# A two-block transformer kernel: a router computed ahead of its norm, 8 KB expert rows, and a final norm applied after the turn

## The chip, the cores and the metric

The kernel runs on one core of a Trainium2 chip. The metric is device time in microseconds (us) of one execution. Engines are named PE (TensorE), DVE (VectorE), ACT (ScalarE) and SP (SyncE, which issues nearly all loads here). POOL does nothing in this kernel.

## The reference, cut to what matters

256 tokens of width 1024, all in float32. A first block has two layers of FFN, three kinds of attention, and FFN. A second block normalizes and modulates, runs attention and retention, and adds the result through `w_out`. What the change touches comes after that:

```
x_new = x + gt1 * (concat([attn_x, ret_x]) @ w_out)
h2 = rmsnorm(x_new, norm2_g) * (1 + sc2) + sh2            # modulated norm
grp_p  = softmax(h2 @ w_grp + b_grp)                      # 4 groups, the best is taken
sel    = (h2 @ w_exp + b_exp) of that group's 8 experts   # 32 experts in all
p_e, j = top_k(softmax(sel), 2)                           # two experts for each token
weights = p_g * p_e / sum(p_e)
y = sum over the two: weight * (silu(h @ w_gate[e]) * (h @ w_up[e])) @ w_down[e]
out = rmsnorm(x_new + gt2 * y, final_norm_g)
```

Each expert has `w_gate` and `w_up` of 1024 x 512 and `w_down` of 512 x 1024, 2 MB each, 201 MB for all 32.

## The kernel before

Activations stand turned, features on partitions: `xT` is 128 x 8 tiles x 256 tokens. Weights come as pieces in a fixed order (`stream_plan`), which SP loads in `stream` (L537 to L561) and PE takes with `take` (L648). Before the experts a piece is 512 KB and there are six places in `W`. From the experts on, `piece_place` gives a ring of 24 places of 512 KB (`RING`): 14 of them over `W`, `WH` and `WL`, which the earlier stages use, and 10 behind the zone. SP fills the ring once ahead of the routing in `first_experts` (L523), as each place comes free. Every further load waits until PE has used the piece 24 places back (`plain_used`), and for the table of which expert each block of 64 slots belongs to (`table_ready`, L598). SP reads an expert's number into a register at its first gate piece (L553).

A gate or up piece holds two of the eight rows of 512 values that each partition needs, 4 KB in one run; a down piece holds 128 rows of 1024 values, 4 KB a partition.

PE, ACT and DVE share four PSUM banks in turns: PE's `begin` waits until DVE gave the bank four turns back, `take` on DVE waits for PE's product (`work_ready`), and `give` frees it. `link` makes DVE wait for its own last operation. Four other banks hold sums over a whole product.

The router's order is serial. All of w_out2's products end, `residual` (L1629) adds them to x, ACT squares (L1279), PE sums over partitions with a matrix of ones (`norm`, L734), ACT takes the root, DVE the reciprocal (L1613) over 256 columns, and 8 + 8 operations (L1616, L1626) scale and shift to `hT`. PE multiplies `hT` with the router's matrix `WR` (L1083, 16 matmuls of 36 columns, each run as two records) and turns `hT` to tokens on partitions (L1091). DVE routes each half of 128 tokens by itself (L2046 to L2083), with an exponential on ACT between (L1484, L1486). Then DVE makes `h2l`, the low part of the turned h2 (L2088), PE counts the tokens of each expert (L1098 to L1103), and DVE works out the blocks of each expert, the expert table (L2115 to L2122), the slot of each token (L2124 to L2139) and the selection matrices of the first four blocks (`select`, L2141). PE gathers the tokens of four blocks with them (`gather`, L1106), DVE copies to `XT` (L2165), and PE turns the weighted selection (`turn_selection`).

The experts run in 16 pairs of blocks. For each pair PE computes gate and up products (`hidden_product`, L1137), adds the pair before back to the tokens in two parts (`scatter`, L1129), turns the hidden values, gathers the next four blocks on every second pair, and computes the down product (`down_product`, L1160). Two blocks of 64 slots lie side by side on PE's columns. Eight more blocks are run only if the table asks for them; in this data it does not.

At the end DVE waits for the last scatter, reads the table's length for the branch (L2197), and goes through residual, norm and scaling to `hT`. PE turns it (L1218), DVE copies four tiles (L2204), and SP stores each (L606).

## Time and profile before

| | |
|---|---|
| median of 3 runs | 2227.05 us (2223.64 to 2229.04) |
| the profiled execution | 2220.84 us, its span 2218.9 us |
| mean granted PE clock | 0.979 |
| PE busy | 2090.0 us (94%), modelled |
| PE weight loads | 1694.3 us (76%) |
| DVE busy | 1187.9 us (54%) |
| ACT busy | 632.8 us (29%) |
| loaded from memory | 467.96 MB |
| DMA packets | 287144, of which 223188 under 2 KB and 286988 under 8 KB |

A busy PE is not PE at its peak: matmuls are pipelined and their ends are modelled, so a wait for data shows only in part. The page's slices show where the load on the DMA engines is; the chain of waits shows what ended last. A share of the DMA just above 1 means that packets overlap on an engine.

### The profile page before, as it was taken

The numbers are of one execution on the slowest core, as the hardware profiler recorded it, in microseconds if no ns is written. First come the engines' busy times: TensorE is split into PE (matmuls) and PEld (weight loads), VectorE is DVE, ScalarE is ACT, GpSimd is POOL, SyncE is SP. The second block draws the span as 40 slices with busy tenths as digits, with TensorE's granted clock in tenths as the row PEclk, the third lists the DMA queues.
The fourth block names the chain that finished last, engine by engine and source line by source line (L and its number), as shares of the span: only waits on it lengthen the run. The fifth ranks groups of instructions, "written<-read, shape, count | busy, mean of one in ns | idle before, by whom it ended". The sixth has DMA issues, their size and how long they took to land.

```text
span 2218.9 us, 33949 instructions
## 1 busy us (share of the span) xinstructions
PE 2090.0 (94%) x14045; PEld 1694.3 (76%) x14045; DVE 1187.9 (54%) x2050; ACT 632.8 (29%) x934; POOL 0.2 (0%) x4
## 2 busy tenths in 40 slices
PE   7999999999999999999999999979893999999997
PEld 7999998779999999999878999968573444334443
DVE  6665658774655655666885555553556222222212
ACT  4433434423333533344441433320321000000000
POOL 0000000000000000000000000000000000000000
PEclk9999999999999999999999999989996999999999
DMA  7966552238866666654233676512321899999994
GB/s 227 281 204 181 169 166 84 86 114 225 263 211 195 196 212 204 181 171 152 67 114 106 229 234 210 164 39 76 133 103 69 333 416 416 415 416 415 416 417 186
DMA packets 287144, 471.36 MB, mean 212 GB/s; under 512 B 17306, under 2 KB 223188, under 8 KB 286988
## 3 DMA queue, kind: packets, MB, share of 16 engines
q1 hardware_dynamic: 285680, 466.19, 61.3%
q10 hardware_dynamic: 1308, 2.96, 0.5%
q8 instruction: 114, 1.87, 0.3%
q14 instruction: 42, 0.34, 0.0%
HBM read 467.96 MB, written 1.13 MB: 211 GB/s over the span
## 4 chain that ended last, share of the span: by engine, by line
PE 82%; DMA 10%; DVE 5%; ACT 1%; issue 1%; SPq 1%; DVEq 0%; ACTq 0%
PE ps L618 81%; DMA ring_zone<-in_moe_w_up_dram 5%; DMA ring_over<-in_moe_w_gate_dram 4%; DMA W<-in_ffn_w_gate_dram 1%; PE ps L903 1%; DVE QK L1838 1%; SPq L556 0%; PE ps L1038 0%; DVE hl L1564 0%; DVE hT L1616 0%; DVE WL L1553 0%; DVE xT L1571 0%; DMA PT<-in_norm_g_dram 0%; PE ps L1156 0%; ACT WH L1243 0%
## 5 line engine op out<-in xcount | busy, mean ns | idle before, releaser
L1553 DVE TENSOR_TENSOR WL<-W,WH 128x1024 fp32r<-128x1024 f32 x372 | 453.0, 1223 | 341.9 <-ACT WH L1243 341.9
L618 PE MATMUL ps<-hh,WH 128*128 128x256 f32 x2128 | 610.1, 287 | 12.2 <-DVE WL L1553 6.6
L618 PE MATMUL ps<-hh,WL 128*128 128x256 f32 x2128 | 601.5, 283 | 0.0
L618 PE MATMUL ps<-hl,WH 128*128 128x256 f32 x2128 | 601.4, 283 | 0.0
L1243 ACT ACTIVATE WH<-W 128x1024 fp32r<-128x1024 f32 x372 | 391.5, 1056 | 496.8 <-PE ps L618 472.6
L618 PEld LDWEIGHTS ps<-hh,WH 128*128 128x128 f32 x2128 | 403.0, 189 | 33.0 <-issue 30.1
L618 PEld LDWEIGHTS ps<-hl,WH 128*128 128x128 f32 x2128 | 402.8, 189 | 0.2
L618 PEld LDWEIGHTS ps<-hh,WL 128*128 128x128 f32 x2128 | 402.8, 189 | 0.0
L618 PE MATMUL ps<-ring_over,XT 128*64 128x512 f32 x896 | 204.7, 596 | 24.4 <-DMA ring_over<-in_moe_w_up_dram 13.3
L618 PE MATMUL ps<-hid_h,WH 128*128 128x256 f32 x704 | 202.9, 288 | 0.0
L618 PE MATMUL ps<-hid_h,WL 128*128 128x256 f32 x704 | 198.7, 282 | 0.0
L618 PE MATMUL ps<-hid_l,WH 128*128 128x256 f32 x704 | 198.5, 282 | 0.0
L618 PEld LDWEIGHTS ps<-ring_over,XT 128*64 128x64 f32 x896 | 65.2, 136 | 160.9 <-issue 159.7
L1501 ACT ACTIVATE sgE<-ps 128x512 f32<-128x512 f32 x16 | 9.6, 597 | 464.0 <-PE ps L618 464.0
L618 PEld LDWEIGHTS ps<-hid_h,WH 128*128 128x128 f32 x704 | 132.9, 189 | 6.3 <-issue 5.8
L618 PEld LDWEIGHTS ps<-hid_l,WH 128*128 128x128 f32 x704 | 132.7, 189 | 0.5
L618 PEld LDWEIGHTS ps<-hid_h,WL 128*128 128x128 f32 x704 | 132.7, 188 | 0.0
L2183 DVE TENSOR_TENSOR hidE<-sgE,ps 128x512 f32<-128x512 f32 x16 | 11.0, 687 | 217.3 <-PE ps L618 217.3
L618 PE MATMUL ps<-yT,W 128*128 128x256 f32 x512 | 116.2, 380 | 0.0
L618 PE MATMUL ps<-ring_zone,hidT 128*64 128x512 f32 x512 | 113.5, 595 | 0.6 <-issue 0.6
L618 PEld LDWEIGHTS ps<-yT,W 128*128 128x128 f32 x512 | 95.0, 190 | 14.4 <-issue 2.8
L618 PEld LDWEIGHTS ps<-ring_zone,hidT 128*64 128x64 f32 x512 | 35.8, 137 | 67.2 <-issue 67.2
(315 smaller groups left out, 2338.4 us busy)
## 6 DMA issues: line engine op xcount, KB each, us to landing
ring_over<-in_moe_w_gate_dram SPq DMA_DIRECT2D x128, 512.0 KB, 14.8
ring_zone<-in_moe_w_down_dram SPq DMA_DIRECT2D x128, 512.0 KB, 15.1
ring_over<-in_moe_w_up_dram SPq DMA_DIRECT2D x96, 512.0 KB, 15.4
W<-in_ffn_w_gate_dram SPq DMA_DIRECT2D x88, 512.0 KB, 5.0
W<-in_ffn_w_up_dram SPq DMA_DIRECT2D x88, 512.0 KB, 4.0
W<-in_ffn_w_down_dram SPq DMA_DIRECT2D x88, 512.0 KB, 3.7
W<-in_w_in_dram SPq DMA_DIRECT2D x78, 512.0 KB, 3.9
W<-in_w_gate_dram SPq DMA_DIRECT2D x48, 512.0 KB, 3.6
```

The costliest lines, as they stand in the source:

```text
L618: ins = nc.tensor.matmul(o, lhsT, rhs, start=start, stop=stop, skip_group_check=True, **kw)
L903: ins = nc.tensor.transpose(bank[:, k * T + q * P:k * T + (q + 1) * P], S[:, u % 4, q * T + k * P:q * T + (k + 1) * P], ident)
L1243: nc.scalar.activation(high, W[:, i % RAW, :], ACT.Copy).then_inc(high_ready, 1)
L1501: nc.scalar.activation(sgE[:, :], bank, ACT.Silu).then_inc(sg_ready, 1)
L1553: v.tensor_tensor(low, W[:, i % RAW, :], high.bitcast(F32), ALU.subtract).then_inc(low_ready, 1)
L1838: give(v.reciprocal(r2, r2))
L2183: v.tensor_tensor(hidE[:, :], sgE[:, :], bank, ALU.mult).then_inc(work_free, 2)
```

## The change

Three parts are changed at once.

**Router.** The norm factor of a token is one number, so the logits can be computed from x before it is known: `logit = r * (x_new @ (G * WR)) + (shift @ WR + b)`. `G` is the column gain of the norm and its modulation. The last term, `LB`, is computed early, beside the first projections. `logits_and_squares` is put between w_out2's products: for the two feature tiles of each PSUM bank it adds 2 matmuls for the logits (turned, 64 columns each, on two column strips) and 2 for the squares (32 columns each, on four strips), as soon as DVE has added that bank to x. A small product with `fold` adds the strips and turns the logits; one-column products with `ones` turn the sum of squares, so the root and reciprocal are over 2 values a partition. ACT scales x to `hT` without the factor; the factor is applied when ACT and DVE copy the turned tiles to `h2h` and `h2l`, and the shift when DVE copies the gathered tiles to `XT`. The shift (`MOD[:, 24:32]`) is needed with the features in another order, and goes through a DRAM scratch. Routing runs both halves of the tokens in one operation where the form allows. The exponentials and weights (`routing_weights`), the expert table (`block_table`) and the weighted half of the selection (`select_weighted`) are moved behind the first gather; the turning of the first weighted selection is moved behind the first pair's hidden values.

**Expert rows.** A piece is 1 MB: four of a partition's eight rows of gate or up (8 KB in one run), or two of its four rows of down, whose rows are now dealt `(p k)` instead of `(k p)`. `hidE` is written in the matching order. The ring has 12 places of 1 MB, 7 of them over the earlier buffers.

**End.** The last scatter signals each PSUM bank, DVE adds and scales bank by bank without the norm factor, PE turns the tiles meanwhile, and the factor is applied by DVE (first half of the tokens) and ACT (second) in the copy out of PSUM.

```
-RING, RING_OVER = 24, 14
+LONG = 2 * PIECE
+RING, RING_OVER, RING_RAW = 12, 7, RAW // 2
...
-            plan.extend((kind, 2 * pair + e, j, 0) for j in range(4) for e in range(2))
+            plan.extend((kind, 2 * pair + e, j, 0) for j in range(2) for e in range(2))
...
-                return w.rearrange("o (p k) n -> p (o k) n", k=KD)[:, 2 * c:2 * c + 2, :]
+                return w.rearrange("o (p k) n -> p (o k) n", k=KD)[:, 4 * c:4 * c + 4, :]
             elif kind == "moe_down":
-                return I["moe_w_down_2"][0, bass.ds(key, 1)].rearrange("o (k p) n -> p (o k) n", p=P)[:, c:c + 1, :]
+                w = I["moe_w_down_2"][0, bass.ds(key, 1)]
+                return w.rearrange("o (p k) n -> p (o k) n", k=HIDDEN)[:, 2 * c:2 * c + 2, :]
...
                     if plan[i] == ("w_in2", 0, 0, 0):
                         sp.dma_start(moe_const[:, :], I["consts"][:, CONST_MOE:]).then_inc(moe_load, 16)
+                        sp.wait_ge(m_ready, KD * DEPTH)
+                        sp.dma_start(mod_scr.rearrange("(k p) -> p k", p=P), MOD[:, 24:32, 0], allow_slow_non_contiguous=True)\
+                            .then_inc(shift_scr, 16)
+                    if plan[i] == ("w_in2", 0, 5, 0):
+                        sp.wait_ge(shift_scr, 16)
+                        sp.dma_start(shift_of[:, :], mod_scr.rearrange("(p k) -> p k", k=KD)).then_inc(shift_load, 16)
...
+            bank = begin()
+            for k in range(KD):
+                mm(bank[0:1, 0:40], MOD[:, 24 + k, 0:1], WR[:, k, :], k == 0, k == KD - 1,
+                   then=work_ready if k == KD - 1 else None)
+            turns.step()
...
+            def logits_and_squares(b):
+
+                if b == 0:
+                    pe.wait_ge(wg_ready, 1)
+                    pe.wait_ge(work_free, turns.n)
+                pe.wait_ge(x2_ready, b + 1)
+                for k in (2 * b, 2 * b + 1):
+                    at = k % 2 * 64
+                    mm(ps[at:at + 64, 0, 0:T], WG[:, k, :], xT[:, k, :], k < 2, k >= KD - 2,
+                       then=lg_ready if k == KD - 1 else None)
+                pe.wait_ge(sq_ready, due(sq_ready))
+                for k in (2 * b, 2 * b + 1):
+                    at = k % 4 * 32
+                    mm(squares[at:at + 32, 0:T], ones[:, 0:32], mT[:, k, :], k < 4, k >= 4,
+                       then=sum_ready if k == KD - 1 else None)
...
                     done_plain()
-            norm()
+                    if half and c:
+                        logits_and_squares(c - 1)
+            logits_and_squares(3)
+            pe.wait_ge(part_ready, due(part_ready))
+            for tt in range(TT):
+                mm(ps[:, 1, tt:tt + 1], rs[:, tt * P:(tt + 1) * P], ones[:, 0:1], tt == 0, tt == 1,
+                   then=sum_ready if tt else None)
+            pe.wait_ge(lc_ready, 1)
+            for tt in range(TT):
+                mm(ps[:, 2, tt * 64:tt * 64 + 40], rstd[:, tt * P:(tt + 1) * P], fold[:, :], tt == 0, tt == 1,
+                   then=lg_ready if tt else None)
...
             def select(quad):
 
+                link(v.tensor_scalar(near[:, :, :], token_slot[:, :, :], float(-QUAD * SLOTS * quad), None, ALU.add))
+                for tt in range(TT):
+                    ins = v.tensor_scalar(Sel_a[:, tt, :], slot_no, near[:, tt, 0:1], None, ALU.is_equal)
+                link(ins)
+                for tt in range(TT):
+                    ins = v.scalar_tensor_tensor(out=Sel[:, tt, :], in0=slot_no, scalar=near[:, tt, 1:2],
+                                                 in1=Sel_a[:, tt, :], op0=ALU.is_equal, op1=ALU.add)
+                ins.then_inc(sel_ready, 1)
...
             def gathered(quad):
 
                 for g in range(4):
                     bank = take()
-                    give(v.tensor_copy(flat(XT[:, quad % 2, 2 * g:2 * g + 2, :]), bank))
+                    for k in (2 * g, 2 * g + 1):
+                        ins = v.tensor_scalar(XT[:, quad % 2, k, :], bank[:, k % 2 * T:(k % 2 + 1) * T],
+                                              shift_of[:, k:k + 1], None, ALU.add)
+                    give(ins)
...
                 select(first // QUAD)
                 gathered(first // QUAD)
-                selection_turned(first // 2)
+                if first == 0:
+                    block_table()
+                    routing_weights()
+                select_weighted(first // QUAD)
...
+            for b in range(4):
+                dve.wait_ge(acc_ready, accs + b + 1)
+                for f in range(2):
+                    k = 2 * b + f
+                    ins = v.scalar_tensor_tensor(out=xT[:, k, :], in0=ps[:, b, f * T:(f + 1) * T],
+                                                 scalar=MOD[:, 40 + k, 0:1], in1=xT[:, k, :],
+                                                 op0=ALU.mult, op1=ALU.add)
+                ins.then_inc(last_x, 1)
+                dve.wait_ge(last_x, b + 1)
+                for k in (2 * b, 2 * b + 1):
+                    ins = v.tensor_scalar(hT[:, k, :], xT[:, k, :], col("final2", k), None, ALU.mult)
+                ins.then_inc(last_scaled, 1)
+            dve.wait_ge(std_ready, 1)
+            v.reciprocal(lamt[:, 0:TT], rstd_of[:, :]).then_inc(last_norm, 1)
+            dve.wait_ge(rows_ready, 2)
+            dve.wait_ge(last_norm, 1)
+            for q in range(2):
+                v.tensor_scalar(otok[:, 0, q * 512:(q + 1) * 512], ps[:, WORK + q, :], lamt[:, 0:1], None, ALU.mult)\
+                    .then_inc(otile, 1)
```

In the routing that replaces L2046 to L2083, DVE's order is: 2 operations `LGE = ps * rtok + LB`; maximum, its index (each for both halves), a cast, the group's one-hot, the product with it and its sum over groups; maximum and index again, a cast, the experts' one-hots, their sum, `chosen`, and two subtractions for the exponentials. Then come `h2l` and the counts as before. The slots take `first`, `own_at`, `slot[:, 0]` in two steps, and two each of pick, reduce and unshift. PE counts with 3 matmuls instead of 5. On PE the first product of a group of four blocks waits for each `XT` bank by itself (`dve_did(x_idx - 3 + k // 2)`) instead of for the last.

## Rows read from the trace of the kernel before

**Rows 1.** The page's slices of 55.5 us, GB/s loaded and stored in each.

```profile
GB/s 227 281 204 181 169 166 84 86 114 225 263 211 195 196 212 204 181 171 152 67 114 106 229 234 210 164 39 76 133 103 69 333 416 416 415 416 415 416 417 186
```

**Rows 2.** Four stretches: busy time, PE clock, DMA share, GB/s.

```profile
1520.00:1560.00 40.00, 40.00 (x185) 34.85 (x184) 7.18 (x11) 0.00 (x0) 0.00 (x0) 1.00 0.24 79
1680.00:1685.00 5.00, 4.88 (x23) 4.88 (x24) 0.06 (x1) 0.00 (x0) 0.00 (x0) 0.50 0.00 0
1690.00:1727.00 37.00, 12.47 (x65) 9.60 (x66) 25.87 (x103) 4.36 (x11) 0.00 (x0) 0.63 0.00 1
1879.00:1940.00 61.00, 55.92 (x269) 24.61 (x268) 14.22 (x34) 1.20 (x2) 0.00 (x0) 1.00 1.03 416
```

**Rows 3.** The chain that ended last, its end: start, us, what.

```profile
2165.01 14.95 DMA ring_zone<-in_moe_w_up_dram
2180.09 3.86 PE ps L618 x16
...
2194.13 3.71 PE ps L618 x16
```

**Rows 4.** PE's timeline, the first down products: start, us, what.

```profile
1739.75 7.09 PE L618 MATMUL ps<-ring_zone,hidT 128*64 128x512 f32 x32 [0.61 <-issue]
...
1768.63 7.09 PE L618 MATMUL ps<-ring_zone,hidT 128*64 128x512 f32 x32
...
1793.69 7.09 PE L618 MATMUL ps<-ring_zone,hidT 128*64 128x512 f32 x32
```

**Rows 5.** Timeline of all engines, 1655 to 1760, from residual to first expert product.

```profile
1666.80 3.23 DVE L1640 SCALAR_TENSOR_TENSOR xT<-ps,MOD,xT 128x256 f32<-128x256 f32 x8 [15.54 <-PE ps L618]
1667.71 0.63 ACT L1279 ACTIVATE mT<-xT 128x512 f32<-128x512 f32 x1 [27.17 <-DVE xT L1640]
...
1672.21 0.47 ACT L1287 ACTIVATE rs<-ps,eps 128x256 f32<-128x256 f32 x1 [1.52 <-PE ps L618]
...
1672.79 1.75 DVE L1613 RECIPROCAL rstd<-rs 128x256 f32<-128x256 f32 x1 [2.76 <-ACT rs L1287]
...
1680.12 7.04 PE L618 MATMUL ps<-WR,hT 128*128 128x36 f32 x32 [7.94 <-DVE hT L1626]
...
1687.19 0.16 DVE L2042 TENSOR_TENSOR LG<-ps,rb 128x4 f32<-128x4 f32 x1 [7.13 <-PE ps L618]
...
1698.14 2.48 DVE L2088 TENSOR_TENSOR h2l<-ps,h2h 128x512 fp32r<-128x512 f32 x4
...
1701.32 0.19 DVE L2095 TENSOR_SCALAR blocks<-ps 128x32 f32<-128x32 f32 x1 [0.56 <-PE ps L618]
...
1704.27 1.48 DVE L2115 TENSOR_TENSOR XT<-scan,moe_const 1x1280 f32<-1x1280 f32 x1
...
1707.65 0.18 DVE L2124 TENSOR_TENSOR first<-scan,blocks 128x32 f32<-128x32 f32 x1
...
1711.24 0.17 DVE L2144 TENSOR_SCALAR near<-token_slot 128x4 f32<-128x4 f32 x1
...
1716.72 0.79 PE L618 MATMUL ps<-Sel,h2h 128*128 128x256 f32 x2 [15.44 <-DVE SelW L2156]
...
1723.42 12.24 PE L618 MATMUL ps<-ring_over,XT 128*64 128x512 f32 x56 [0.56 <-DVE XT L2165]
```

**Rows 6.** SP's queue, the first loads that need the table.

```profile
1727.27 5.49 SPq L556 DMA_DIRECT2D ring_over<-in_moe_w_gate_dram  x8
```

**Rows 7.** Timeline of the end, 2160 to 2219.

```profile
2199.34 3.23 DVE L1640 SCALAR_TENSOR_TENSOR xT<-ps,MOD,xT 128x256 f32<-128x256 f32 x8 [5.36 <-issue]
...
2213.86 2.89 SPq L606 DMA_DIRECT2D out_dram<-mT  x4
...
2215.70 0.69 DVE L2204 COPY mT<-ps 128x512 f32<-128x512 f32 x1 [0.16 <-PE ps L1218]
```

**Rows 8.** Timelines of the second block's first norm and of w_out2.

```profile
1452.32 6.52 PE L618 MATMUL ps<-mT,ones 128*128 128x256 f32 x16 [3.24 <-ACT mT L1279]
...
1638.97 27.79 PE L618 MATMUL ps<-yT,W 128*128 128x256 f32 x128
```

More of the change, by code:

```diff
@@ L1007, in _ @@
                     side(kind, piece)
+                if g == 8:
+                    pe.wait_ge(lrow_ready, 1)
+                    bank = begin()
+                    mm(bank[:, 0:40], ones[0:1, :], lrow[:, :], True, True, then=work_ready)
+                    turns.step()
             t_idx, pv_idx = {}, {}
@@ L1073, in _ @@
                                yT[:, k, :], half + f + j == 0, k == KD - 1,
-                               then=acc_ready if half and c == 3 and f and j == 3 else None)
+                               then=acc_ready if half and f and j == 3 else None)
                     done_plain()
-            norm()
-            pe.wait_ge(h_ready, due(h_ready, KD))
-            bank = begin()
-            for tt in range(TT):
-                for k in range(KD):
-                    last = tt == TT - 1 and k == KD - 1
-                    mm(bank[:, tt * 64:tt * 64 + 36], hT[:, k, tt * P:(tt + 1) * P], WR[:, k, :],
-                       k == 0, k == KD - 1, then=work_ready if last else None)
-            turns.step()
+                    if half and c:
[9 more added lines that the diff above has]
+                   then=lg_ready if tt else None)
+            pe.wait_ge(h_ready, due(h_ready, KD))
             for j in range(4):
@@ L1191, in experts @@
                     t_idx = turn_hidden()
+                    if pair == first // 2:
+                        turn_selection(pair)
                     if y_idx is not None:
@@ L1409, in _ @@
             turns.step(4)
+            turns.step()
             norm(xT)
@@ L1442, in _ @@
                     side(kind, piece)
+                turns.step(g == 8)
             def decay(h):
@@ L1496, in experts @@
                 turns.step(4)
-                turns.step()
                 for pair in range(first // 2, last // 2):
@@ L1502, in experts @@
                     turns.step(3)
+                    turns.step(pair == first // 2)
                     if more and pair % 2 == 1:
@@ L1896, in _ @@
                 v.tensor_copy(rt[:, 0, b:b + 1], eps[:, :]).then_inc(x_tiles, 1)
+            bank = take()
+            give(v.tensor_copy(lrow[:, :], bank[0:1, 0:40]))
+            given()
+            v.tensor_copy(rt[:, 1, 0:1], eps[:, :]).then_inc(lrow_ready, 1)
             link(scaled(xT[:, :, :], hT[:, :, :]))
@@ L1971, in _ @@
                     side(kind, piece)
+                if g == 8:
+                    bank = take()
+                    give(v.tensor_tensor(LB[:, :], bank[:, 0:40], rb[:, :], ALU.add))
+                    given()
             def decay_arg(h):
```

409 lines of the change are left out of this document (259 added, 150 removed).

## The prediction

> **What bounds the kernel now.** I read the slices of the page first: from slice 33 to slice 39 the core loads 415 to 417 GB/s without a break [rows 1]. The table by stage says how close that is to full: in a stretch of 61 us the DMA share is 1.03 at 416 GB/s while TensorE's modelled busy time is 55.9 us [rows 2]. The chain of waits then shows that the DMA really ends last: it runs through the landing of a piece in each pair, the last one 14.95 us long to 2179.96, and PE works only the last 16 matmul records after it [rows 3]. PE alone could go faster: with pieces in store, three starts of the down product lie 28.88 and 25.06 us apart, 53.9 us a quad against 61 us by DMA [rows 4]. So the expert stage is worth its bytes divided by the rate, plus what lies in front of it and behind it. In front: from the end of the w_out2 products (1666.8) to the first expert product (1723.42) is 56.6 us of one serial chain [rows 5], and between 1690 and 1727 the DMA share is 0.00 [rows 2], since the ring is full and no slot comes free before PE eats a piece; the first new issue is at 1727.27 [rows 6]. A microsecond saved in that chain is therefore a microsecond of the end. Behind: from the last scatter (2194.13 + 3.71 = 2197.84) to 2218.9 is 21.1 us of small steps [rows 3, 7].
>
> **The sum is made against the profiled execution,** 2220.84 us (span 2218.9); the median of the three runs is 2227.05, so 6.2 us are added at the end, by subtracting the saving from the median.
>
> **Router, before.** 56.6 us [rows 5]: 13.3 us of residual, squares, factor and norm to 1680.12; 7.0 us for 16 logit matmuls (32 records); 10.95 us for the routing of two token halves (1687.19 to 1698.14, some 54 short DVE operations, 0.20 us each with the two ACT trips); 3.2 us of h2l; 2.95 us of block counts; 3.4 us of expert table; 3.6 us of slots (16 operations, 0.22 each); 5.5 us of selection; 6.7 us of gather with the last XT copy.
>
> **Router, after.** (a) The residual, squares and logits of bank b now follow w_out2's own bank b. Two groups (b = 0, 1) stand in PE's queue ahead of the last w_out2 products. A group is 4 matmuls; a w_out2 matmul of the same 256 columns is 27.79/64 = 0.43 us [rows 8]; the four sit on separate column strips, as the expert products do, which take 12.24/28 = 0.44 us for 512 columns [rows 5], half of what 0.43 at 256 gives. So 0.9 us a group (1.7 if strips don't overlap), +1.8 us. The group b = 2 lies beside the residual of bank 3. (b) From there to the logits: 2 residual operations 0.85 (3.23/8 each [rows 5]), square 0.7, two ones products 0.55, copy out 0.55, two one-column products 0.6, root 0.35, reciprocal and wait 0.35, with sizes from the steps they replace: together 4.1 us, between 3 and 6. The 1.75 us reciprocal over 256 columns, the 16 norm operations and the 7.0 us of logits are gone. (c) Routing is 22 operations with both halves in each step, at 0.20 us: 4.5 us (3.3 if unlinked neighbours overlap). The exponentials leave the path. (d) h2l still stands ahead of the counts on DVE, 3.2 us; counts 2.95. PE's transposes and ACT's four scaled copies lie beside the routing; without that cover 2 us more. (e) The table moves behind the gather: 0 here. (f) Slots 10 operations at 0.22: 2.2 us. (g) Selection is one `near` and four operations of 256 columns near 0.42 us (the same STT costs 0.40 on PSUM [rows 5]): 1.9 us, as the weighted half is moved behind the gather too. (h) Gather 5.9 us [rows 5]; the product starts on the first XT banks, so the last copy is not waited for. Sum: 1.8 + 4.1 + 4.5 + 3.2 + 2.95 + 2.2 + 1.9 + 5.9 = 26.6 us. **Saving 30 us,** between 26 and 33. The granted clock was 0.50 in this stretch [rows 2], the 1.2 GHz level; the gather's price contains it, and I count on no better.
>
> **What the move costs.** SP waits for the table, which DVE now makes after the XT copies: about 1.0 + 3.4 us after the product's start, and a slot of 1 MB comes free only after 8 products (3.5 us) instead of 4. Issue today is 3.85 us after the start (1723.42 to 1727.27 [rows 5, 6]), of which 1.75 is the products, so about 2 is SP's own way. After: 4.4 + 2 = 6.4 us. SP then gives 2 MB at once where before it gave 0.5 MB pieces, so of these 2.6 us I count 1.4 (0 to 3). Nothing but expert loads is queued there. The routing weights and the weighted selection (some 6 us of DVE) must be ready for the transposition of the first pair, 14 us after the start: hidden. The bias row adds 8 products with one stationary column ahead of the norm at 1452.32, whose 6.52 us are on the path [rows 8]; the bound is 16 records at 0.22 us = 3.5, the least near 0.5: +2, and 0.4 for the second small product. The shift's way through DRAM is 8 elements a partition while SP is several pieces ahead: 0 (1 at most).
>
> **The 8 KB rows.** The stream from restart to the last up piece brings 352 pieces of 0.52 MB, 184.5 MB; counted from 1730.6, where a full-rate stream would have had to begin, to 2179.96 [rows 3] it is 449.4 us. What does a longer row give? At 4 KB rows a full share carries 416/1.03 = 404 GB/s; in a stretch with 1 KB rows alone, 79 GB/s at 0.24, it is 329 [rows 2]. With 16 engines that is 162 ns and 50 ns a packet, so 37.5 ns a KB and 12 ns fixed; 8 KB would take 312 ns instead of 324, 3.8% less. That is one bound (16.4 us); the other is no gain, if 416 is already what the port takes. I take 2.6%, two thirds of the way, as the fixed part was seen between 1 and 4 KB and nothing shows it gone: **11.4 us.** PE's 53.9 us a quad stay under the 59.5 that this gives.
>
> The Trainium skill (DMA: Bandwidth & Descriptors, Why small descriptors are slow) puts the fixed cost at about 3 fabric cycles a packet, and its ceiling is 435 GB/s. By it 4 KB to 8 KB gives 1.2%, 5 us, and a time near 2188; the trace's 12 ns a packet speaks for more than 3 cycles.
>
> **Tail of the stream.** After the last up pieces land PE has 8 products instead of 4: +1.75 us; against it the down product today waits 0.5 us for its last piece and won't: +1.3.
>
> **The end, before:** 21.1 us: 1.5 until DVE starts at 2199.34, then residual, squares, root, reciprocal, scaling, transposes and copies one behind another to 2216.4, four issues of 0.72, and 2.15 from the last issue (2216.75) to the end of the span [rows 7]. **After:** the branch on the table is taken while PE scatters, and acc is given bank by bank, so DVE starts 2.3 us before the scatter ends and does a bank in 1.5 us: the last x is ready 2.9 us after it; square 0.7, squares product 0.6, copy 0.6, small products 0.6, transposes of the last bank 0.9: 6.4; scaled copy 0.75; the third and fourth issue follow at 0.72 steps to 9.4; from there to the end 2.5: 11.9. **Saving 9 us** (7 to 10).
>
> **Total:** -30 + 1.4 + 2.4 - 11.4 + 1.3 - 9 = -45.3. 2227.05 - 45.3 = 2181.8, say **2182 us** (profiled near 2175.5).
>
> **Rivals.**
> 1. The rate doesn't rise (packets are cut to 4 KB, or 416 is the port): 2182 + 11.4 = 2193. For it: the flat 415 to 417 [rows 1] looks like a ceiling. Against: the price per packet above. 18%.
> 2. The coarser ring makes PE and DMA take turns. With 12 slots of 1 MB, each pair does 4 more products after its last up piece; if that delays the reissue on which the stream hangs, 16 pairs lose 1.75 us each, 28 us: 2210. Against: in the 10 us that PE is behind, some 4.5 MB land of 12.6, so the queue never runs dry. 7%.
> 3. The other side, slower: the long rows are served worse than 4 KB ones, as one engine now holds each piece up for longer. All else being won (33.9 us), this decides from 449.4/(449.4 + 33.9) = 0.93 of the rate, 387 GB/s; at 380 GB/s it is 2236. No row shows a longer row going slower; 1 KB to 4 KB went the other way [rows 2]. 3%.
> 4. More than forecast (3.8% and a router at 24 us): 2166. 4%.
>
> My own case holds 68%, 2170 to 2190. **Range** 2170 to 2197: it takes in rival 1 and leaves out 2, 3 and 4. All but rival 3 are faster by over 0.3% (6.7 us, about what three runs here can tell from no change): faster 0.96, same 0.01, slower 0.03.
>
> **What the profile would show.** Right: first expert product 25 to 29 us after the last w_out2 product; LGE within 5 us of it; GB/s near 427 over whole slices and packets of 8 KB; last store about 12 us after the last scatter. Wrong: GB/s still 416; SP's first table-dependent issue over 8 us after the first product; PE idle on DMA for longer than now with the DMA share under 1; a wait of the counts on h2h.

## The result, and the profile after

The changed kernel takes 2166.61 us, the median of 4 runs (2160.68 to 2170.63), against 2226.98 us (4 runs, 2223.64 to 2229.04) for the kernel before beside it: a ratio of 0.9727, 95% interval 0.9706 to 0.9749. It is faster by 60.4 us. The forecast was 45 us, 2182, and its range ended at 2170. The profiled execution took 2166.41 us; its span, 2164.6, is 54.3 us shorter than before's. The other 6 us of the 60.4 are not in the two profiles: before's profiled execution (2220.84) was 6.2 us under its own median, and under every other execution of that kernel on record (2221.03 to 2231.11), while after's is at its median. Where a good part of them went is shown behind experiment 15.

The stages, from the two traces (us):

| stretch | before | after | difference | forecast |
|---|---|---|---|---|
| start to the end of the first block | 1446.6 | 1435.7 | -10.9 | 0 |
| to the start of w_out2's products | 192.4 | 194.5 | +2.1 | +2.4 |
| w_out2's start to the first expert product | 84.5 | 53.6 | -30.8 | -30 |
| first expert product to the last `hidE` | 458.7 | 453.0 | -5.7 | -8.7 |
| to the end of the last scatter | 15.7 | 15.5 | -0.2 | 0 |
| last scatter to the end | 21.1 | 12.2 | -8.9 | -9 |

The stream is the stretch from the first expert product to the last `hidE`; its forecast is -11.4 for the rows, +1.4 for the restart and +1.3 for the tail. Two rows are not as forecast, in opposite directions: the first block gave 10.9 us that nobody had asked for, and the stream gave 3 less.

**The router.** The timeline of the changed kernel, all engines, answers to [rows 5]:

```profile
1656.95 3.72 PE L652 MATMUL ps<-yT,W 128*128 128x256 f32 x16
...
1660.71 0.88 DVE L2164 SCALAR_TENSOR_TENSOR xT<-ps,MOD,xT 128x256 f32<-128x256 f32 x2 [3.92 <-PE ps L652]
...
1661.74 0.65 PE L652 MATMUL ps<-xT,PT 128*64 128x256 f32 x4
...
1663.00 0.38 ACT L1575 ACTIVATE rs<-ps 128x256 f32<-128x256 f32 x1 [0.74 <-PE ps L652]
...
1664.63 0.43 DVE L2175 SCALAR_TENSOR_TENSOR LGE<-ps,rtok,LB 128x40 f32<-128x40 f32 x2
...
1668.47 2.60 DVE L2241 SCALAR_TENSOR_TENSOR h2l<-ps,rtok,h2h 128x512 fp32r<-128x512 f32 x4
...
1670.99 0.18 DVE L2248 TENSOR_SCALAR blocks<-ps 128x32 f32<-128x32 f32 x1
...
1673.93 0.19 DVE L2265 TENSOR_TENSOR first<-scan,blocks 128x32 f32<-128x32 f32 x1
...
1675.73 0.17 DVE L2325 TENSOR_SCALAR near<-token_slot 128x4 f32<-128x4 f32 x1
...
1677.52 0.80 PE L652 MATMUL ps<-Sel,h2h 128*128 128x256 f32 x2 [6.81 <-DVE Sel L2330]
...
1683.83 10.94 PE L652 MATMUL ps<-ring_over,XT 128*64 128x512 f32 x49
```

Read the starts one after another. From the last w_out2 product (1660.67) the last residual, squares, sums, root and reciprocal lead to `LGE` in 4.0 us (forecast 4.1). The routing of both halves together, up to `h2l`, is 3.84 us, where two halves one after the other were 10.95. Counts, slots and selection follow to 1677.52, and the gather to 1683.83 is 6.3 us. Before, the same stretch from w_out2's last product was 56.6 us; it is 23.2 now, and w_out2 itself grew from 27.79 to 30.46 us because the logits and squares of two banks stand among its products.

**The restart.** SP's queue, the first loads that need the table, answers to [rows 6]:

```profile
1689.39 3.40 SPq L581 DMA_DIRECT2D ring_over<-in_moe_w_gate_dram  x4
```

That is 5.56 us after the first product (1683.83), where it was 3.85.

**The stream.** The page's slices of loaded GB/s, the window of 61 us (as in [rows 2]), and the end of the chain that ended last (as in [rows 3]), all of the changed kernel:

```profile
GB/s 226 276 218 178 164 184 98 88 88 193 282 216 201 200 225 216 176 158 185 103 92 78 195 243 215 195 73 78 79 97 175 315 422 420 421 421 421 421 421 252
```

```profile
1879.00:1940.00 61.00, 55.84 (x274) 26.37 (x272) 16.36 (x39) 1.19 (x2) 0.00 (x0) 1.00 1.01 421
```

```profile
2108.00 24.93 DMA ring_zone<-in_moe_w_up_dram
2133.06 5.58 PE ps L652 x24
2139.08 8.77 PE ps L652 x40
...
2148.71 1.12 PE ps L652 x4
```

The rate rose from 416 to 421, not to 427. The last up piece now stands for 24.93 us in that chain instead of 14.95, and DMA is 17% of the chain instead of 10%: this stage is bound by DMA before and after. PE's part behind the last landing is 24 records instead of 16, as a coarser piece must leave.

**The end.** The timeline of the changed kernel's last 15 us, beside [rows 7]:

```profile
2149.85 0.88 DVE L2405 SCALAR_TENSOR_TENSOR xT<-ps,MOD,xT 128x256 f32<-128x256 f32 x2 [1.29 <-PE ps L652]
...
2157.70 0.38 ACT L1615 ACTIVATE rs<-ps 128x256 f32<-128x256 f32 x1 [2.00 <-PE ps L652]
...
2159.08 0.17 DVE L2414 RECIPROCAL lamt<-rstd_of 128x2 f32<-128x2 f32 x1 [3.39 <-ACT rstd_of L1617]
...
2160.13 1.88 SPq L640 DMA_DIRECT2D out_dram<-mT  x4
```

DVE starts on the first bank 2.55 us before the last scatter ends (2152.40), where before it waited for all of it, and the first store is issued 7.7 us behind the scatter instead of 16.0.

**The first block.** The diff puts nothing into it before the bias row. Yet three long unbroken stretches of PE, of the same count of records, are shorter. They stand in the chain that ended last; first the kernel before, then the changed one:

```profile
564.34 164.94 PE ps L618 x1421
734.79 204.58 PE ps L618 x1745
...
1193.48 252.55 PE ps L618 x1962
```

```profile
563.81 161.94 PE ps L652 x1421
731.26 201.13 PE ps L652 x1745
...
1186.19 248.89 PE ps L652 x1962
```

The windows over the first of them (busy times, clock, DMA share, GB/s), before and after:

```profile
564.40:729.00 164.60, 164.60 (x1421) 160.28 (x1422) 98.69 (x114) 61.98 (x63) 0.00 (x0) 1.00 0.71 218
```

```profile
564.00:725.00 161.00, 161.00 (x1417) 156.72 (x1417) 98.53 (x114) 61.99 (x63) 0.00 (x0) 1.00 0.73 223
```

PE never waits in either, the granted clock is 1.00 in both, and the DMA has room: so it is not a clock, a wait or a load. It is 3.0, 3.45 and 3.66 us, 1.4 to 1.8%, for the same instructions with the same operands. What did change for them is where their operands lie: the router's new small buffers are allocated in front of `hl`, and push `hl`, `hh` and everything in the zone 1184 B up in each partition. (`hh` and `hl` are the high and low part of the activations, which stream through PE as the moving operand; `WH` and `WL` are the same of the weights, the stationary operand; `hid_h` and `hid_l`, the hidden values, lie in the zone.) The experiments had to settle this, and why the stream gave less than forecast.

### The profile page after: what moved, and what is told of

It reads as the page before. It is cut to its first block, busy times and chain, and to the rows that moved or that the text cites. A ratio compares the mean times of both kernels' runs of the same rounds, so it can differ in the third digit from the quotient of the medians.

```text
span 2164.6 us, 33353 instructions
## 1 busy us (share of the span) xinstructions
PE 2062.4 (95%) x14055; PEld 1676.9 (77%) x14055; DVE 1181.1 (55%) x2009; ACT 637.2 (29%) x942; POOL 0.2 (0%) x4
## 4 chain that ended last, share of the span: by engine, by line
PE 77%; DMA 17%; DVE 4%; ACT 1%; issue 1%; SPq 0%; DVEq 0%; ACTq 0%
PE ps L652 75%; DMA ring_zone<-in_moe_w_up_dram 15%; DMA W<-in_ffn_w_gate_dram 2%; PE ps L937 1%; DVE QK L1949 1%; PE ps L1082 0%; DVE hl L1674 0%; DVE WL L1663 0%; DVE xT L1681 0%; ACT WH L1324 0%; DMA PT<-in_norm_g_dram 0%; SPq L581 0%; DVE xT L1726 0%; DVE yT L1952 0%; DVE xT L1861 0%
## 5 line engine op out<-in xcount | busy, mean ns | idle before, releaser
L1663 DVE TENSOR_TENSOR WL<-W,WH 128x1024 fp32r<-128x1024 f32 x372 | 453.0, 1223 | 337.7 <-ACT WH L1324 337.7
L652 PE MATMUL ps<-ring_over,XT 128*64 128x512 f32 x896 | 228.4, 595 | 30.2 <-DMA ring_zone<-in_moe_w_up_dram 13.6
L652 PEld LDWEIGHTS ps<-ring_over,XT 128*64 128x64 f32 x896 | 77.7, 137 | 174.9 <-issue 174.5
L2379 DVE TENSOR_TENSOR hidE<-sgE,ps 128x512 f32<-128x512 f32 x16 | 16.8, 1048 | 205.0 <-PE ps L652 205.0
L652 PE MATMUL ps<-yT,W 128*128 128x256 f32 x512 | 116.7, 381 | 0.0
```

The costliest lines, as they stand in the source:

```text
L652: ins = nc.tensor.matmul(o, lhsT, rhs, start=start, stop=stop, skip_group_check=True, **kw)
L1663: v.tensor_tensor(low, W[:, i % RAW, :], high.bitcast(F32), ALU.subtract).then_inc(low_ready, 1)
L2379: v.tensor_tensor(hidE[:, :].rearrange("p (k m) -> p m k", k=HIDDEN), by_row(sgE[:, :]), by_row(bank), ALU.mult).then_inc(work_free, 2)
```

## The experiments

"First block" ends at the reciprocal of its closing norm; "stream" is from the first expert product to the last `hidE`. Each ratio is to the kernel before on the same chip.

**1. The expert rows alone** (the kernel before with the second part of the change).

```
-RING, RING_OVER = 24, 14
...
+LONG = 2 * PIECE
+RING, RING_OVER, RING_RAW = 12, 7, RAW // 2
...
-                return w.rearrange("o (p k) n -> p (o k) n", k=KD)[:, 2 * c:2 * c + 2, :]
+                return w.rearrange("o (p k) n -> p (o k) n", k=KD)[:, 4 * c:4 * c + 4, :]
```

> The kernel before with the 8 KB expert rows and the ring of 12 places alone; router, end and all buffers in front of the zone are as before. Theory A (the rows are worth what the two traces show in that stage: rate 416 to 421 GB/s, first expert product to the last up piece landed 456.5 to about 448 us, tail 1.6 us longer): about 6 us faster, 2221 against 2227, first block unchanged (final_g norm starts at about 1446.6). Theory B (as predicted, 2.6% more rate): 9 to 10 us faster. Rival C (the coarse ring costs what the long rows give): within 2 us of before. If the first block gets 10 us faster here too, the ring or the piece order is what speeds it up.

Measured: 2216.02 us, ratio 0.9963 (0.9949 to 0.9977). The stream takes 448.6 us, 10.1 less than before, at these rates (the page's slices):

```profile
GB/s 223 276 207 187 165 171 86 86 103 208 274 212 192 199 215 203 180 166 169 77 86 114 201 247 214 189 31 84 144 38 134 271 425 425 425 425 425 426 425 192
```

So alone the rows gave more than in the full change, and more than the 8.7 net of the forecast. SP's first load came here 5.56 us after the first product too (1727.53 to this row of SP's queue), with the table still made early:

```profile
1733.09 3.40 SPq L559 DMA_DIRECT2D ring_over<-in_moe_w_gate_dram  x4
```

The later restart is therefore the coarser piece's, and not the moved table's.

**2. The end alone.**

```
-            residual(lambda k: MOD[:, 40 + k, 0:1], waited=True)
-            norm(xT, hT, lambda k: col("final2", k), last=True)
...
+            for b in range(4):
+                dve.wait_ge(acc_ready, accs + b + 1)
...
```

> The kernel before with the new end alone. Theory A: last scatter to the end of the span goes from 21.1 to about 12.2 us, 9 us faster, 2218, nothing else moves. Rival: part of the gain belongs to the shorter router (clock, DVE state), then under 7 us.

Measured: 2217.95 us, ratio 0.9966 (0.9952 to 0.9980). From the last scatter to the end 12.2 us against 21.1: the whole term, alone. The medians say 7.6 us, between 4.5 and 10.7 by the interval, which takes in the stage's 8.9.

**3. The change without the expert rows.**

```
-LONG = 2 * PIECE
-RING, RING_OVER, RING_RAW = 12, 7, RAW // 2
+RING, RING_OVER = 24, 14
```

> The changed kernel with the 4 KB rows and the ring of 24 places of before. Theory A (the parts add, and the first block's 10.9 us come with the buffers that the router part adds): about 2173, first block ends its last FFN at about 1435.7, router stretch about 31 us shorter than before, expert stream about 456 us as before. Rival C (rows cost or give nothing): 2167, as the changed kernel. Rival D (the first block's gain comes with the ring): 2184, first block as before.

Measured: 2179.41 us, ratio 0.9792 (0.9775 to 0.9808). From w_out2's start to the first expert product 53.6 us, end 12.2, first block 1436.2. But the stream is 467.4 us, longer than before's 458.7 although its loads are the same. The two surprises are both here, without the long rows. I had expected 456 us for the stream and 2173 in all.

**4. Only the places.** The kernel before with 294 unused floats in front of `hl`; not one instruction changes.

```
+        sb("pad", [P, 294])
         hl = sb("hl", [P, KD, T], FR)
```

> The kernel before with one unused buffer of 294 values a partition (1176 B) ahead of hl and the zone, which is the sum by which the changed kernel's new buffers move them. No instruction changes. Theory A (the place of hl, hh and the zone in the partition sets how fast PE reads, or how it collides with DVE and ACT): about 10 us faster, all in the first block's FFNs (1421 matmul records of the second FFN in 162 us instead of 165). Rival E (the first block's gain is a difference between executions, chips or the clock): no change, within 3 us of 2227. Rival F (it comes from something else in the changed program, such as the DRAM layout or the router's loads): no change either, but e3 shows it.

Measured: 2216.66 us, ratio 0.9958 (0.9943 to 0.9972): unused bytes make the kernel 9 us faster. The chain that ended last has the changed kernel's stretch:

```profile
563.76 161.93 PE ps L619 x1421
```

The first block is 1435.5 us, 11 shorter than in before's profile. The stream is 465.7 us, 7 longer, at this rate in the window of 61 us:

```profile
1879.00:1940.00 61.00, 55.16 (x266) 24.42 (x264) 14.20 (x34) 1.19 (x2) 0.00 (x0) 1.00 1.03 409
```

That settles both surprises as matters of place. The two stages together give only 4 us, though, where the medians (2216.66 and 2224.74) give 8 and the ratio 9. The rest is that before's profiled execution, 2220.84, was shorter than its runs beside this one.

**5 to 7. Which buffer, in small steps.** The kernel before: with 32 B in front of `hl` and the zone kept on its multiple of 256 B (it moves by a whole 256 B); with `hl` kept and the zone moved 32 B; with 64 B in front of all of them. One run each.

```
+        sb("pad", [P, 8])                       # 5, and 56 floats behind hl; 7: [P, 16]
         hl = sb("hl", [P, KD, T], FR)
+        sb("pad", [P, 8])                       # 6, behind hl
```

> The kernel before with hl alone moved by 32 B in the partition (so that it starts 32 B into a 64 B line) and everything behind it on 64 B lines as before. Theory A1 (the FFNs' gain comes from where PE's moving operand hl lies): the last FFN ends at about 1435 instead of 1446 to 1453, the expert stream keeps 458 to 459 us. Theory A2 (it comes from the zone, hh and the hidden values): first block as before, stream as before.

> The kernel before with the zone alone (hh, the hidden values, ring_zone) moved by 32 B, hl as before. Theory A2: last FFN ends near 1435 and the expert stream (first product to the last hidden product) is 465 to 467 us, since ring_zone is off its 64 B line. Theory A1: last FFN as before, 1446 to 1453, and the stream still 465 to 467 us. If both halves count, the FFN gain is split between this run and the one of hl.

> The kernel before with hl and the zone moved by 64 B, so that they stay on 64 B lines but leave the 256 B ones. If only the place within 64 B counts: first block as before (1446 to 1453) and stream 458 to 459 us. If the place within 256 B counts: a gain in the first block or a loss in the stream here too.

Measured: 2216.79, 2229.47 and 2208.05 us, beside 2224.59 (one run) for the kernel before. The stretch of 1421 records takes 163.87, 163.53 and 161.61 us (before 164.94), the first block 1444.3, 1449.3 and 1428.5. `hl` and the zone each have a part in it, as far as single runs tell. My theory behind these runs, that a start off a 64 B line makes the gain, fell: the move by 64 B keeps all on such lines and gains most. The stream is 458.4 us in the first, where `ring_zone` is back on a multiple of 256 B, and 465.8 and 464.4 in the others, where it is 32 and 64 B behind one.

**8. The changed kernel with `hl` and `ring_zone` on 64 B lines** (192 B behind a multiple of 256).

```
+        sb("pad", [P, 8])
         hl = sb("hl", [P, KD, T], FR)
```

> The changed kernel with 32 B of padding ahead of hl, so that hl and the zone lie on 64 B lines again. If the place within 64 B is the whole of it: last FFN ends at 1446 to 1451 instead of 1435.7 and the expert stream goes from 453.0 to 448.6 us, as with the rows alone (e1); in all some 7 us slower than the changed kernel, near 2173. Rival (the first block's gain needs only a move from where it was): still 1436, stream 448.6, near 2162.

Measured: 2171.59 us, one run. First block 1442.2 (the stretch of 1421: 163.37), stream 452.8. A line of 64 B does nothing for the stream either.

**9. The changed kernel with `ring_zone` on a multiple of 256 B.**

```
-            ("ring_zone", [P, RING - RING_OVER, LONG], F32))
+            ("pad", [P, 24], F32), ("ring_zone", [P, RING - RING_OVER, LONG], F32))
```

> The changed kernel with one difference: 96 unused bytes in front of ring_zone, so that the five ring places behind the zone begin on a multiple of 256 B in the partition. hl, hh and the zone stay where they are. Theory that the place of the DMA's destination sets the stream: from the first expert product to the last hidE it takes 448.6 us, as in the rows-only kernel, against 453.0 in the changed kernel; nothing else changes, first block 1435.7; time 4.4 us under the changed kernel, near 2162. Rival, that the lost 4.4 us belong to the router and end in the same kernel (more work on PE and DVE beside the stream): the stream stays at 453, time 2166.

Measured: 2158.76 us (4 runs), ratio 0.9709 (0.9687 to 0.9732). The stream is 448.3 us against 453.0, as the first theory said, and the slices show 425 GB/s as in experiment 1. In the medians the intervals of this kernel and the changed one overlap, so the gain rests on the stage. In this profile w_out2's start also comes 3.7 us sooner after the first block. That is the clock: from 1455 to 1630 us the granted clock is 0.95 here and 0.93 in the changed kernel, and 0.02 of 175 us are 3.5 us.

**10. Both places.** As 9, with `hl`, `hh` and the zone at the 64 B offset of experiment 7; the row `lrow` moves into an unused part of `rt`, so that it takes no place of its own.

```
-        lrow = sb("lrow", [1, 40])
+        lrow = rt[0:1, 14:16, :].rearrange("p a n -> p (a n)")[:, 0:40]
+        sb("pad_hl", [P, 16])
         hl = sb("hl", [P, KD, T], FR)
...
+            ("pad", [P, 48], F32), ("ring_zone", [P, RING - RING_OVER, LONG], F32))
```

> The changed kernel with its buffers placed by what the runs so far show: ring_zone on a multiple of 256 B, and hl, hh and the zone with the 64 B offset of the fastest first block seen. Theory, that both gains are of the places alone and add up: first block 1428.5 to 1430 (1435.7 in the changed kernel), stream 448.6, time 2154 to 2157. Rival, that the first block's time follows from something else that differed in that kernel: first block stays at 1435.7, time 2162.

Measured: 2155.16 us, ratio 0.9682 (0.9660 to 0.9703). The chain's stretch repeats experiment 7 to the hundredth:

```profile
565.43 161.61 PE ps L653 x1421
```

Stream 449.0. But the first block is 1432.6, only 1.2 below experiment 9 and 4 above experiment 7: TensorE's rate in these stretches is a matter of the places; the length of the whole block is not that alone (see behind experiment 15).

**11. Long pieces, short rows.** The kernel before with pieces of 1 MB and the ring of 12, each partition's bytes from two places in memory.

```
+                return w.rearrange("o (p a c i) n -> p (o a) c (i n)", a=2, c=2, i=2)[:, :, c, :]
...
+                return w.rearrange("o (k p) n -> p (o k) n", p=P)[:, 2 * c:2 * c + 2, :]
```

> The kernel before with the changed kernel's 1 MB pieces and its ring of 12, but each partition's bytes come as two runs of 4 KB from two places in memory, so packets stay at 4 KB. ring_zone is on a multiple of 256 B. Theory, that the length of the packet sets the rate: stream 458.7 us as before or a little more, since PE's grouping of four adds up to 1.4 us; time 2225 to 2227. Rival, that half as many DMA instructions and waits of SP make the gain: stream 448.6 us, time 2216. If the coarser ring had a price of its own (the rival of 7 per cent in the prediction), it shows here bare: over 462 us.

Measured: 2226.40 us, ratio 1.0010 (1.0000 to 1.0020), stream 459.1 us. Its page, slices and packets:

```profile
GB/s 224 274 213 180 162 170 86 86 105 215 272 209 191 206 211 207 176 168 161 68 107 111 217 238 212 170 38 76 132 91 80 319 417 416 416 416 416 416 417 190
DMA packets 284067, 471.31 MB, mean 212 GB/s; under 512 B 14234, under 2 KB 220116, under 8 KB 283916
```

Same pieces, same ring, same issues as experiment 1, which has 234764 packets under 8 KB: 416 instead of 425 GB/s. So the long packet, with the long run in memory that makes it, is the whole gain, and the coarse ring costs 0.4 us, nothing.

**12. All moved by 128 B.**

```
+        sb("pad", [P, 32])
         hl = sb("hl", [P, KD, T], FR)
```

> The kernel before with 128 unused bytes in front of hl, so that hl, hh, the zone and ring_zone all begin 128 B behind a multiple of 256 B. If the rate of the expert stream wants a destination on 256 B and not only on 128 B, the stream takes 464 to 466 us as with 64 B; if 128 B is enough, 458.5. For the first block, one more point on what the place does to matmuls: offsets of 0, 64 and 160 B gave 1446.6, 1428.5 and 1435.5 us. If it follows the distance to the weights' buffers (WH begins 128 B behind a multiple of 256), 128 B puts both on the same offset and gives an extreme, slower than 1446 or faster than 1430; if it is no matter of 256 B at all, something between.

Measured: 2234.88 us, ratio 1.0051 (1.0034 to 1.0069): 128 unused bytes make it 11 us slower. Stream 465.5, so 128 B is not enough for it; and the chain's stretch is the slowest of all:

```profile
569.46 166.11 PE ps L619 x1421
```

**13 to 15. Place or distance, and the other part of the ring.** All kernels so far have `W`, `WH`, `WL` and, over them, `ring_over` 128 B behind a multiple of 256. In 13 every buffer moves by 64 B; in 14 every buffer by 128 B, with `ring_zone` kept on its multiple; 15 does the same to the kernel of experiment 10.

```
+        sb("pad_all", [P, 32])                  # 16 in experiment 13
         with nc.sbuf_tensor("ring_over", [P, RING_OVER, PIECE], F32) as ring_over:
```

> The kernel before with 64 unused bytes in front of the first buffer, so that every buffer moves by 64 B and all distances stay. If TensorE's rate in the first block follows from the place of hl, hh and the zone alone, its stretch of 1421 records takes 161.6 us, as with the 64 B in front of hl; if it follows from their distance to WH and WL, 164.94 us as before. Stream: ring_zone and ring_over both off a multiple of 256 B (64 and 192), so 464 to 466 us if only that counts.

> The kernel before with 128 unused bytes in front of the first buffer and 128 more in front of ring_zone: ring_over and ring_zone now both begin on a multiple of 256 B, and hl, hh and the zone keep their distance to WH and WL. If distance counts for TensorE, the stretch of 1421 records takes 164.94 us; if place, 166.11 us. Stream, in the kernel before 458.7 us: if ring_over's 14 places cost by the same measure as ring_zone's 10 (7 us), it takes about 449 us and the time is 2214 with 164.94 or 2224 with 166.11; if loads over ring_over cost nothing by their place, 458.7.

> The kernel best_places with 128 more unused bytes in front of the first buffer, ring_zone staying on its multiple of 256 B: now ring_over is on one too, and hl is 192 B behind one, at the same distance to WH as in best_places. If distance counts for TensorE, the stretch of 1421 records stays at 161.61 us; if place, 163.4 us. Stream, 449.0 us in best_places: if ring_over's 7 of 12 places cost as ring_zone's 5 did (4.5 us), it falls by 6 us to 443, unless PE's own 53.9 us for four blocks or another limit shows first; time near 2149. If they cost nothing: 449, time 2155.

Measured: 2234.41 us (one run); 2219.01 us, ratio 0.9982 (0.9972 to 0.9991); 2145.15 us, ratio 0.9647 (0.9631 to 0.9663), the fastest kernel of this study and 3.5% under the kernel before. The chains' stretch in 13, 14 and 15:

```profile
567.92 165.05 PE ps L619 x1421
```

```profile
566.64 164.95 PE ps L619 x1421
```

```profile
556.81 161.61 PE ps L654 x1421
```

With all distances kept it is before's 164.94 again, wherever the buffers lie, and with experiment 10's distances 161.61. So TensorE's rate does not follow the place of `hl`, `hh` and the zone but their distance to the buffers in front of them. Of those PE reads only `WH` and `WL` in these stretches. That these two are the ones that count is argued; no run moved them alone.

One rival can be looked up in the traces: that PE collides with what DVE, ACT or the DMA write beside it. I took the time from the start of one of these matmuls to the start of the next, between 570 and 718 us, over some 1150 pairs in each trace (steps over 150 ns left out). The mean is 119.0 ns in the kernel before, 116.7 in the changed one, 116.6 in experiment 7 and 119.9 in experiment 12. Over the pairs beside which neither DVE nor ACT works (66 to 94 of them) it is 119.1, 117.3, 117.1 and 120.0; over those with no DMA packet under way (110 to 144), 119.0, 116.7, 116.4 and 120.0. So the difference is in PE's own pace and needs no other engine. The small moves show one thing more. In experiment 5 the step from a matmul that reads `hh` to one that reads `hl` fell most, from 118.8 to 116.4 ns; from `hl` to `hh` it was 118.6 (before 119.0). In experiment 6 it was the other way round (118.1 and 116.8). So how two successive moving operands lie to each other counts as well.

The stream takes 466.0, 454.5 and 446.7 us. So `ring_over` costs by its place as well, though less than the 10 and 6 us that I expected: 4.2 in experiment 14 and 2.3 in 15. The windows of 61 us of 14 and of 15:

```profile
1879.00:1940.00 61.00, 56.54 (x272) 25.14 (x271) 14.20 (x34) 1.19 (x2) 0.00 (x0) 1.00 1.03 419
```

```profile
1879.00:1940.00 61.00, 55.95 (x274) 26.67 (x273) 15.42 (x34) 1.20 (x2) 0.00 (x0) 1.00 1.01 426
```

**The clock beside the places.** Before's profile and experiment 1's have the same instructions and the same places in the first block, and its 1421 records take 164.94 us in both. Yet they start 4.0 us later in experiment 1 (568.32 against 564.34). Most of it arises where the granted clock fell behind a stretch in which PE had little to do (busy for 1.33 of the 5 us from 440 on in the kernel before). The window over it, before and in experiment 1 (PE clock third from the end):

```profile
440.00:460.00 20.00, 16.33 (x90) 12.51 (x90) 18.73 (x39) 7.20 (x22) 0.00 (x0) 0.91 0.24 79
```

```profile
440.00:460.00 20.00, 16.33 (x68) 12.10 (x66) 16.67 (x35) 5.73 (x16) 0.00 (x0) 0.74 0.24 79
```

So I added up, for each trace, the time from 22 us to the end of the first block at the lower of the two clocks (0.50, 1.2 GHz):

| distance of `hl`, `hh` and the zone | us at the lower clock: first block, us (experiment) |
|---|---|
| as before | 10: 1446.6 (before); 17: 1448.9 (14), 1450.8 (1); 20: 1450.9 (11); 24: 1452.8 (13); 27: 1453.5 (2) |
| 160 B more | 14: 1433.8 (9); 17: 1435.5 (4), 1435.7 (changed), 1436.2 (3) |
| 64 B more | 17: 1428.5 (7), 1424.6 (15); 27: 1432.6 (10) |

Before's profile is the one with the least of it, by luck of the execution. With 17 us in all of them, the shift by 160 B is worth 13 to 15 us in the first block and not 11, and the 64 B 20 to 22. The table also accounts for the gap between experiments 10 and 7, 4 us at 10 us more of the lower clock. Experiment 15 is 8 us under 10, about half of it by the same 10 us. The other half, 4.0 against experiment 7, may be the weights now loaded to multiples of 256 B: ACT waits 15.1 us for the loads of `w_gate` ahead of 560 us, and 18.4 in experiment 7. In experiment 14, 1.9 under experiment 1, it could be the same; single traces don't settle it.

## Why the prediction was off

**What failed** is a term that the prediction put at nothing without a reason: the first block. It costed the change instruction by instruction and took that block's time as fixed, since hardly an instruction changes there. But the change brings new small buffers, and the prediction never asked where they push the old ones. Experiment 4 shows it: the shift alone makes the first block 11 us shorter than in before's profile, and takes 7 us in the stream. The miss is 15.1 us. The table's differences from the forecast add up to 9, of which the first block is 10.9; the other 6.2 are the distance of before's profiled execution to its median. A good part of those 6.2 is the same block: in five other traces with before's distances it takes 2.3 to 6.9 us longer than in before's profile, with more time at the lower clock. At an equal 17 us of it the shift is worth 13 to 15 us there. Without the shift, 8 to 9 us in all by experiment 4, the time would have been about 2175, inside the range.

**The 8 KB rows** (forecast -11.4, 427 GB/s): the size was about right for a ring as it stood before. Experiment 1 has -10.1 for the stream as a whole, against a net forecast of -8.7, at 425 GB/s. In the changed kernel it was cut to -5.7 because `ring_zone` had moved off its multiple of 256 B; experiment 9 brings it back (448.3). Laid out by length and place:

| stream, us | both rings on 256 B | `ring_over` off | both off |
|---|---|---|---|
| packets of 4 KB | 454.5 | 458.1 to 459.1 | 464.4 to 467.4 |
| packets of 8 KB | 446.7 | 448.3 to 449.0 | 452.8 to 453.0 |

The price of a bad place is 10 to 13 us with 4 KB packets and 6 us with 8 KB: it is paid by the packet. The packets' own times say so too (means over 1879 to 1940 us): a 4 KB packet takes 159.2 ns with both rings on 256 B (experiment 14) and 163.3 with both off (4), an 8 KB packet 309.5 (15) and 313.9 (the changed kernel), 4.1 and 4.4 ns more. And the price of the short packet is 7.8 us with both rings well placed (1.7%), 10 with the ring as before, 11 to 15 with both off. The forecast's 12 ns of fixed cost came from a trace with 14 of 24 ring places off a multiple of 256 B. Two 4 KB packets less one of 8 KB are 8.9 ns with all places on it and 12.7 with all off. In experiment 1 an 8 KB packet took 310.6 ns, where the forecast's price gives 312 and two 4 KB packets took 321 before: 3.3% less. The rate rose by only 2.2%, while the DMA share, in which packets overlap on an engine, fell from 1.03 to 1.01. So the price per packet was read rightly; that two thirds of it would arrive as rate was a guess that came close, and why the share fell isn't shown. The Trainium skill (DMA: Bandwidth & Descriptors, Why small descriptors are slow), quoted in the prediction, gives 1.2% as an estimate from its 3 cycles; the runs show 1.7% with all places on 256 B and 2.2% as the ring stood, so the measurement decides for more. The same page (How a descriptor splits into AXI transactions) says that a transaction must start on a 256 B boundary, so that a descriptor which does not gets one more, partly wasted. The runs agree in kind: `ring_zone` at 32, 64, 128 and 160 B behind a multiple of 256 gives 464.4 to 467.4 us with 4 KB packets, and at 160 and 192 B 452.8 and 453.0 with 8 KB, so only a multiple of 256 is free. The page counts reads; here it is the writing end that moved.

**The router** (-30, measured -30.8) held term by term: 4.0 us to `LGE` for 4.1, 3.84 of routing for 4.5, 6.3 of gather for 5.9, w_out2 +2.7 for +1.8. **The bias row** (+2.4): the stretch grew by 2.1, but this agreement shows nothing. In experiments 9, 10 and 15, which have the row as well, the stretch takes 190.8 to 191.1 us, less than before's 192.4. What differs is the clock at least: from 1550 to 1600 us it is 0.90 before, 0.83 in the changed kernel and 0.86 in experiment 9. The row's own price isn't shown. **The end** (-9, measured -8.9) held, and alone as well.

**The restart** (+1.4) had its size about right and its reason wrong. I gave it to the table's move behind the gather; experiment 1 has the same 5.56 us with the table early, and experiment 3 has 5.4 with the table late and pieces of 512 KB. Either alone brings it to that, and the two don't add up.

**The rivals.** That the rate doesn't rise is refuted by experiments 1 and 11 together. That the coarse ring makes PE and DMA take turns has no price (459.1 against 458.7). That long rows are served worse has the wrong sign. The fourth, more than forecast, named a time of 2166 that is the one measured, but by a router at 24 us and 3.8% of rate, neither of which came: the router took 25.8 us (23.2, and 2.7 more in w_out2), and the rate rose by 1.2%. That the number fits is luck.

**What stays open:** why the distance between the operands' buffers changes TensorE's rate. Against the distance before, shifts of 0, 64, 128, 160 and 192 B gave 164.9, 161.6, 166.1, 161.9 to 162.3 and 163.4 us for 1421 records. I have no rule that yields this order. Open too are some 4 us of experiment 15's first block.

## What to carry to other kernels

A change that adds or resizes a buffer moves every buffer behind it: print the start of each before and after, and when a stage that the diff doesn't touch gets faster or slower, first run the old kernel with nothing but the unused bytes. Destinations of a DMA-bound stream belong on a multiple of 256 B in the partition, above all with packets of 4 KB; it costs some unused bytes and was worth 2 to 13 us here. Forecast against the profiled execution, but look where it lies among its runs, and compare the granted clock stretch by stretch before crediting a stage with a few us: 6 us of this miss were there before any reasoning began.

## What was not expected of the hardware

- TensorE's long stretches, at a granted clock of 1.00 and without a wait, run 161.6 to 166.1 us for the same 1421 records, 2.8% apart, by nothing but the distance between buffers. Kernels that share it agree within 0.35 us (164.94 to 165.05 in six; 161.61 in three; 161.93 to 162.26 with 160 B). The step from one matmul to the next is 119.0 ns against 116.7, with the other engines busy or idle. Moved by 64 B together, `hl`, `hh` and the zone made the kernel 16.5 us faster (one run); by 128 B, 11 us slower.
- The load rate in the expert stage was 409, 416 and 419 GB/s with 4 KB packets, and 421, 425 and 426 with 8 KB, by the place of the destination: both parts of the ring off a multiple of 256 B, one, none. An ill-placed packet took some 4 ns more, whether of 4 or 8 KB.
- Writing `hidE` in a strided order took 1.05 us instead of 0.69, 16 times, and cost nothing that the stages show, since DVE is idle around it:

```profile
2136.86 1.05 DVE L2379 TENSOR_TENSOR hidE<-sgE,ps 128x512 f32<-128x512 f32 x1 [17.88 <-PE ps L652]
```
